# The last normalisation of a decoder layer: statistics moved to ScalarE, scale and shift fused on VectorE, GpSimd taken out

## What the reference computes

```
def layer_norm(x, g, b):
    mu = jnp.mean(xf, -1, keepdims=True)
    var = jnp.mean(jnp.square(xf - mu), -1, keepdims=True)
    return ((xf - mu) * lax.rsqrt(var + LN_EPS) * g + b)
...
    f = hier_moe(h, w_group, b_group, w_router, b_router, w_gate, w_up, w_down)
    x = layer_norm(DEEPNORM_ALPHA * x + (1.0 + gt2) * f, ln2_g, ln2_b)
```

## Time and profile before

| what | value |
|---|---|
| median of 3 runs | 670.6 us (668.86 to 671.66) |
| profiled execution, its own time | 670.94 us |
| span of the profiled execution | 669.2 us |
| mean granted TensorE clock | 0.91 |
| busy: TensorE | 541.9 us (81%) |
| busy: VectorE | 231.8 us (35%) |
| busy: ScalarE | 151.6 us (23%) |
| busy: GpSimd | 146.7 us (22%) |

### The profile page before, as it was taken

One profiled execution on the slowest core, in us unless ns is written; L12 is line 12 of the kernel. 1 busy time (PEld: TensorE's weight loads), 2 busy tenths in 40 slices (PEclk: granted clock), 3 DMA queues, 4 the chain that ended last, 5 costly groups with the idle time before them and its releaser, 6 DMA issues.

```text
span 669.2 us, 7214 instructions
## 1 busy us (share of the span) xinstructions
PE 541.9 (81%) x2420; PEld 274.1 (41%) x2421; DVE 231.8 (35%) x540; ACT 151.6 (23%) x312; POOL 146.7 (22%) x194
## 2 busy tenths in 40 slices
PE   1879999999989799860099899899999979688560
PEld 0457777886534344430033333334333323233220
DVE  0342444325394397987011111111111111111395
ACT  1222344516373012320011111111111101111021
POOL 5020010000554320202511211121121111111085
PEclk9979999999799799975589999999999979889685
DMA  8993946202828711129289949169999999985611
GB/s 286 408 362 114 345 158 227 92 1 110 308 104 325 226 63 64 65 90 423 84 314 406 419 162 365 65 246 418 418 421 419 419 421 419 417 347 187 256 63 65
DMA packets 46004, 168.97 MB, mean 253 GB/s; under 512 B 13178, under 2 KB 22450, under 8 KB 30590
## 3 DMA queue, kind: packets, MB, share of 16 engines
q1 hardware_dynamic: 36682, 146.48, 56.0%
q0 software_dynamic: 8944, 21.87, 9.2%
q10 hardware_dynamic: 340, 0.09, 0.1%
HBM read 165.18 MB, written 18.32 MB: 274 GB/s over the span
## 4 chain that ended last, share of the span: by engine, by line
PE 61%; DVE 14%; DMA 9%; SPq 8%; issue 4%; ACT 2%; POOL 1%; POOLq 0%; DVEq 0%
PE B L1672 17%; PE B L1424 15%; PE B L1691 8%; PE B L1588 6%; DMA wex<-in_w_up 4%; SPq L370 3%; PE B L1361 3%; SPq L372 2%; DMA x_tok<-in_x_sample 2%; PE B L1493 2%; SPq L369 2%; DVE bn L1135 2%; DVE yy L1329 1%; PE B L1653 1%; PE B L1436 1%
## 5 line engine op out<-in xcount | busy, mean ns | idle before, releaser
L1672 PE MATMUL B<-wex,XT 128*64 128x512 f32 x640 | 152.7, 627 | 18.4 <-DMA wex<-in_w_up 9.9
L1424 PE MATMUL B<-hT,win 128*128 128x256 f32 (+1 forms) x448 | 103.4, 391 | 2.0 <-DVE hT L958 2.0
L1672 PEld LDWEIGHTS B<-wex,XT 128*64 128x64 f32 x640 | 52.6, 144 | 116.4 <-issue 115.2
L1424 PEld LDWEIGHTS B<-hT,win 128*128 128x128 f32 x448 | 85.7, 194 | 22.2 <-issue 9.2
L1691 PE MATMUL B<-wex,zT 128*64 128x512 f32 x320 | 73.1, 598 | 0.6
L1302 DVE TENSOR_TENSOR z<-silu_g,B 128x256 f32<-128x256 f32 x20 | 8.4, 421 | 164.2 <-ACT silu_g L848 164.2
L1588 PE MATMUL B<-wout,yT 128*128 128x512 f32 x112 | 51.5, 619 | 0.0
L1653 PE MATMUL B<-ident,X 128*128 128x128 f32 x168 | 28.4, 294 | 26.8 <-DMA X<-h_dram,gidx 26.8
L617 POOL COPY sidx<-idx_all 128x1 int32 (+1 forms) x20 | 3.6, 181 | 201.2 <-DVE yo L1307 201.2
L848 ACT ACTIVATE silu_g<-B 128x256 f32<-128x256 f32 x20 | 7.7, 383 | 155.7 <-PE B L1672 155.7
L1307 DVE COPY yo<-B 128x512 f32<-128x512 f32 x20 | 13.8, 692 | 83.1 <-PE B L1691 83.1
(11 more groups left out here) (324 smaller groups left out, 602.6 us busy)
## 6 DMA issues: line engine op xcount, KB each, us to landing
wex<-in_w_gate SPq DMA_DIRECT2D x32, 1024.0 KB, 16.8
wex<-in_w_up SPq DMA_DIRECT2D x32, 1024.0 KB, 19.4
wex<-in_w_down SPq DMA_DIRECT2D x32, 1024.0 KB, 20.9
ada<-in_w_ada POOLq DMA_DIRECT2D x12, 1024.0 KB, 7.0
ada<-in_w_ada SPq DMA_DIRECT2D x8, 1024.0 KB, 7.7
win<-in_w_in SPq DMA_DIRECT2D x7, 1024.0 KB, 13.4
wout<-in_w_out SPq DMA_DIRECT2D x1, 4096.0 KB, 13.1
yy<-y_dram SPq DMA_DIRECT2D x8, 512.0 KB, 7.1
```

The source lines that it names most:

```text
L1424: last = pe.matmul(B[(q % 2) * 2 + h][:, 0:cn], win[:, n % 3, k, col:col + P], hT[:, k, c0:c0 + cn], start=(k == 0), stop=(k == KD - 1))
L1672: last = pe.matmul(B[2 + j % 2][64 * q:64 * q + 64, :], XT[:, j % 2, k, 64 * q:64 * q + 64], gu[:, :, k, :], start=(k == 0), stop=(k == KD ...
```

## The change

Behind the weighted sum the work of a tile is divided anew:

- VectorE: gate and residual as before, under the name `gated_sum`. `layer_norm_stats` is no longer called here.
- ScalarE, `row_stats`: the row sum (a Copy of the tile into the spare half `yy[:, t, 1, :]`, with an accumulated sum as second output), minus the mean (a Copy of one column), the sum of squared deviations (Square with minus the mean as bias, accumulated), and the standard deviation (Sqrt with the epsilon as bias). The results have a place for each tile, in `st2`.
- VectorE, `scaled`: the reciprocal, then (f - mean) times `ln2_g` in one pass, then that times the reciprocal plus `ln2_b` in a second one, into `yout`.
- VectorE's order is now gated_sum(0), gated_sum(1), scaled(0), gated_sum(2), scaled(1), gated_sum(3), scaled(2), gated_sum(4), scaled(3), scaled(4).
- GpSimd has nothing to do behind `experts_done`. The normalising pass of ScalarE is gone.

```
+        st2 = small("st2", [P, TT + 1, 4])
+        eps2 = small("eps2", [P, 1])
...
-            pool.wait_ge(lnp_in, 96)
-            for t, n in TILES[:TT]:
-                f = yy[0:n, t, 0, :]
-                pool.wait_ge(xhat_ready, TT + 2 + t)
-                link(pool.tensor_tensor(f, f, mod[0:n, 3, :], ALU.mult))
-                if t >= 2:
-                    pool.wait_ge(out_done[t % 2], 16 * (t // 2))
-                pool.tensor_tensor(yout[0:n, t % 2, :], f, mod[0:n, 4, :], ALU.add).then_inc(out_ready, 1)
...
-            def xhat2(t, n):
+            def row_stats(t, n):
+                f, spare = yy[0:n, t, 0, :], yy[0:n, t, 1, :]
                 act.wait_ge(var_ready, TT + 2 + t)
-                act.activation(st1[0:n, 1:2], st1[0:n, 0:1], ACT.Sqrt).then_inc(std_ready, 1)
-                act.wait_ge(norm_ready, TT + 2 + t)
-                act.activation(yy[0:n, t, 0, :], yy[0:n, t, 0, :], ACT.Identity, scale=st1[0:n, 2:3],
-                               bias=st1[0:n, 3:4]).then_inc(xhat_ready, 1)
+                link(act.activation(spare, f, ACT.Copy, accum_out=st2[0:n, t, 0:1]))
+                link(act.activation(st2[0:n, t, 1:2], st2[0:n, t, 0:1], ACT.Copy, scale=-1.0 / D))
+                link(act.activation(spare, f, ACT.Square, bias=st2[0:n, t, 1:2], accum_out=st2[0:n, t, 0:1]))
+                act.activation(st2[0:n, t, 2:3], st2[0:n, t, 0:1], ACT.Sqrt, scale=1.0 / D, bias=eps2[0:n, :]).then_inc(std_ready, 1)
...
-                link(dve.scalar_tensor_tensor(out=f, in0=x_tok[0:n, t, :], scalar=ALPHA, in1=f, op0=ALU.mult, op1=ALU.add))
-                layer_norm_stats(f, n, TT + 1 + t)
-            dve.wait_ge(xhat_ready, 2 * (TT + 1))
-            link(dve.tensor_tensor(f, f, mod[0:NS, 3, :], ALU.mult))
-            dve.wait_ge(out_done[0], 16 * (TT // 2))
-            dve.wait_ge(out_ready, TT)
-            dve.tensor_tensor(yout[0:NS, 0, :], f, mod[0:NS, 4, :], ALU.add).then_inc(out_ready, 1)
+                settle()
+                dve.scalar_tensor_tensor(out=f, in0=x_tok[0:n, t, :], scalar=ALPHA, in1=f, op0=ALU.mult, op1=ALU.add).then_inc(var_ready, 1)
+
+            def scaled(t, n):
+                f = yy[0:n, t, 0, :]
+                dve.wait_ge(std_ready, TT + 2 + t)
+                link(dve.reciprocal(st2[0:n, t, 3:4], st2[0:n, t, 2:3]))
+                link(dve.scalar_tensor_tensor(out=f, in0=f, scalar=st2[0:n, t, 1:2], in1=mod[0:n, 3, :],
+                                              op0=ALU.add, op1=ALU.mult))
+                if t >= 2:
+                    dve.wait_ge(out_done[t % 2], 16 * (t // 2))
+                dve.scalar_tensor_tensor(out=yout[0:n, t % 2, :], in0=f, scalar=st2[0:n, t, 3:4], in1=mod[0:n, 4, :],
+                                         op0=ALU.mult, op1=ALU.add).then_inc(out_ready, 1)
+
+            for t, n in TILES:
+                gated_sum(t, n)
+                if t:
+                    scaled(*TILES[t - 1])
+            scaled(*TILES[TT])
```

More of the change, by code:

```diff
@@ L864, in _ @@
                     turn(i, False)
-            def xhat2(t, n):
+            def row_stats(t, n):
+                f, spare = yy[0:n, t, 0, :], yy[0:n, t, 1, :]
                 act.wait_ge(var_ready, TT + 2 + t)
-                act.activation(st1[0:n, 1:2], st1[0:n, 0:1], ACT.Sqrt).then_inc(std_ready, 1)
-                act.wait_ge(norm_ready, TT + 2 + t)
-                act.activation(yy[0:n, t, 0, :], yy[0:n, t, 0, :], ACT.Identity, scale=st1[0:n, 2:3],
-                               bias=st1[0:n, 3:4]).then_inc(xhat_ready, 1)
-            for t in range(TT + 1):
-                xhat2(*TILES[t])
+                link(act.activation(spare, f, ACT.Copy, accum_out=st2[0:n, t, 0:1]))
[3 more added lines that the diff above has]
+            for t, n in TILES:
+                row_stats(t, n)
         @block.vector
@@ L1320, in _, with gated_sum @@
                     dve.tensor_scalar(wdiag[0:n, t, c, 0:n], ident[0:n, 0:n], wt[0:n, t, c:c + 1], None, ALU.mult).then_inc(wdiag_ready, 1)
+            step(dve.memset(eps2[:, :], LN_EPS))
             dve.wait_ge(lnp_in, 96)
-            for t, n in TILES:
+            def gated_sum(t, n):
                 f = yy[0:n, t, 0, :]
```

## The result

| what | before | after |
|---|---|---|
| median of 6 runs, us | 669.34 | 663.04 |
| ratio, 95% interval | | 0.9898 (0.9877 to 0.9919) |
| profiled execution, us | 670.94 | 662.54 |
| span, us | 669.2 | 660.5 |

A second comparison (experiment 6) gave 0.9899 (0.9866 to 0.9933). Occasional much slower executions are left out of all ratios and medians.

What follows compares the result with a forecast made beforehand. VectorE was taken as the limit from 634.80 to 663.71; its last pass would end at 660.50, 3.21 us earlier, with 5.49 us behind it unchanged. Forecast 667.5 us, 0.46% less, range 665.9 to 669.6.

Steps and rivals of the forecast that it cites:

- The 5.49 us stay.: Behind VectorE's last pass: the last store lands (2.6 us) and the program ends, 5.49 us in all, unchanged.
- Rival (e): Program's end: something behind VectorE sets it, so the change does not shorten the chain, 670.6 us; chance 0.03.
- cycle: VectorE's time for one tile after the change: 5.19 us, against 4.84 and 5.73 before.
- fused passes: VectorE's two passes per tile in `scaled`: 1.28 us each, as in the first normalisation.
- residuals: VectorE's residual instruction: 1.22 to 1.25 us in all five tiles, without the lengthening of about 0.9 beside GpSimd.
- wait at tile 0: VectorE waits about 0.8 us for ScalarE before tile 0's reciprocal.
- at tile 4: VectorE waits 0.3 us for ScalarE before tile 4's reciprocal.
- Rival (b): ScalarE's accumulated passes are slower than built, up to 3.44 us a tile, giving 668.6 us; chance 0.12.
- The table load: ScalarE's activation table load moves between tile 0's Square and Sqrt, adding 1.32 us on tile 0 alone.
- rival (a): ScalarE, tile 0: switching tables costs more than its load, 2.53 us in place of 1.32, giving 668.7; chance 0.09.
- Rival (c): ScalarE, tile 0: the table load starts early and is hidden, 0.9 us more gained, 666.6 us; chance 0.08.
- Rival (d): ScalarE's SBUF traffic delays VectorE's fused passes as GpSimd did, 7.2 us in all, 674.7 us; chance 0.04.

Runs made afterwards that it cites:

- experiment 6: The changed kernel as it is, run again beside the kernel before: 662.79 us, ratio 0.9899.
- Experiment 1: The changed kernel plus one GpSimd memset of one column that waits for VectorE's last output pass: 669.66 us, ratio 1.0008 to the kernel before.
- experiment 5: The kernel before, with tile 3's two GpSimd passes put on VectorE ahead of tile 4's: 668.05 us, ratio 0.998.
- experiment 3: The changed kernel plus four GpSimd additions of 1024 columns into a scratch tile, from tile 0's residual on: 667.49 us, ratio 0.9956 to the kernel before.

## Why the prediction was wrong

**The failed step** is one sentence of the sum: "The 5.49 us stay." They became 2.19. I had named 2.6 us of the 5.49, the landing of the last store, and let the other 2.9 pass as the program's end. Even the 2.6 was not this store's: the earlier trace rows have it for the four stores of 512 KB, while the last store, of 32 KB, had landed by the time SyncE was through at 665.7, 2.0 us behind the last pass. So 3.5 us were unexplained. They had an owner, GpSimd's closing drain, which ends 7.2 us behind GpSimd's last instruction. The change took GpSimd's last pass from 661.38 to nowhere, and SyncE's wait for the store became the end. Experiment 1 puts the drain back and loses the gain; experiment 5 lets it end earlier and gains, though VectorE ends later. Rival (e) stood next to this, an end set behind VectorE, but I looked for it among the stores and priced it at no change; it was instead a cost that the change removed.

**The change on VectorE** was right and right in size: 25.73 us where 25.70 was forecast. Its parts: cycle 5.18 (5.19 forecast), fused passes 1.28 (1.28), residuals 1.21 to 1.23 (1.22 to 1.25), wait at tile 0 0.91 (0.8), at tile 4 0.34 (0.3).

**ScalarE**: a tile from 642.21 to 645.20, 2.99 us (2.91 forecast), 4.28 with the load (4.23). Rival (b) falls.

**The table load**: rival (a) falls, with 0.02 us between the load and the next activation. The Trainium skill's further drain for a switch (ScalarE: Activation LUTs, What ACT_TABLE_LOAD costs) did not appear here. Rival (c) falls too: the load stood in its place in the order, and moving it removed the wait.

**Rival (d)** falls: the fused passes kept their 1.28 us with ScalarE's passes beside them; beside GpSimd's passes they took up to 3.25 (experiment 3).

**The chances**: 0.38 stood on faster by over 0.5%, 0.57 on within. With the drain's 3.3 us in the sum the forecast would have been 670.94 - 3.21 - 3.30 = 664.4 by the profiled execution. That execution lay 1.6 us above the median of the six runs, which covers the remaining 1.4 us to 663.04.

## What to carry to other kernels

Account for every microsecond behind the last busy instruction: name the row that ends it, on every engine, the closing drains included, before calling it fixed. An engine off the chain of work can still hold the end of the program, so here GpSimd's last instruction had to end at least 7.3 us before the last store had landed to cost nothing; in experiment 5 it ended 10 us before, and its drain was over in time. When work leaves GpSimd, count three things: its own time, the waits it imposed on VectorE's passes, and its drain.

## What was not expected of the hardware

GpSimd's drain ended 7.2 to 7.3 us behind its last instruction whether that was a pass of 2.34 us (before, and experiment 5), one of 3.21 (experiment 3) or a single column (after, and experiment 1, there behind 38 us of idleness). What it waits for is open; it wasn't tried in a program whose GpSimd issues no transfers. On the other engines the drains ended with the last instruction: VectorE's, of 1.31 us after the change, starts with its last pass of 1.27.
